# Three product kinds in three passes: the order of the matmuls in a split-precision weight unit

## The chip, the core and the metric

The kernel runs on one core of a Trainium2 chip. Its engines are TensorE (PE, matrix products, with its weight loads listed as PEld), VectorE (DVE), ScalarE (ACT), GpSimd (POOL) and SyncE (SP, which issues the DMAs). The metric is the device time of one execution in microseconds. Matrix products read their operands from SBUF, the on-chip memory, and write to PSUM banks.

## The reference

Two transformer-like blocks, one after the other, on 256 tokens of width 2048, all in float32. Cut to its matrix products:

```python
def first_block(x, ...):
    h = rms_norm(x, mix_norm)
    parts = split(h @ w_in)                    # inputs of three mixers, and gates
    y_a, y_b, y_c = s5_mixer(...), hgrn2_mixer(...), mlstm_mixer(...)
    merged = sum(sigmoid(g_i) * (y_i @ w_branch_i))
    x = x + merged @ w_out
    x = x + conv_ffn(rms_norm(x, ffn_norm), ffn_w_up, ffn_conv_w, ffn_conv_b, ffn_w_down)
    return rms_norm(x, final_norm)

def second_block(x, ...):
    proj = rms_norm_2(x, g_mix) @ w_in         # inputs of two attentions, and gates
    x = x + (g[0] * (o_a @ w_o_mla) + g[1] * (o_b @ w_o_dil)) @ w_o
    gt, up = split(rms_norm_2(x, g_ffn) @ w_gate_up)
    return x + (silu(gt) * up) @ w_down
```

The up projections have 88 column tiles of 128 (5632 x 2), the down projections 44 tiles of depth.

## The kernel before

Activations lie transposed in SBUF, 16 tiles (KT) of 128 features by 256 tokens. Weights are streamed through a ring of four slots (RING). One "unit" is the 16 tiles of 128x128 that give one output tile of 128 features; its result is accumulated in one PSUM bank. SP loads a slot when PE has signalled `consumed` for it.

Part of the products are made in a split form. A float32 weight w is rounded to `w_high` (a reduced format, fp32r) by ACT in `round_weights` (line 909, copy at line 913; semaphore `rounded`), and the rest, `w_low` = w - `w_high`, is written over the slot by DVE (`lower_weights`, line 1303) or in a few cases by POOL (semaphore `lowered`). The activations have a high and a low part as well. For each tile PE then adds three products to the bank, in `mm3` (line 486): high weight with high activation, high weight with low activation, low weight with high activation. That is 48 matmuls for one unit, each with a weight load of its own. ACT and DVE prepare weights two units ahead of PE (AHEAD).

Split units come from `unit_split` (line 465), called with a body that `project_split` (line 493) makes. It is used for the first 10 units and 6 rounds of four of the mixers' projection, for w_out (4 rounds), for the up projection (4 units and 21 rounds), for the first 26 units of the second block's input projection (in2), for w_o (4 rounds), and for the second up projection (4 units and 21 rounds): 268 units. The projections that give tokens by features (`tokens`, line 522) and the down projection (`down`, line 586) have loops of their own, with the three products of a tile together.

The unit after a norm is special (`after_norm`, line 504): mix, up, in2 and up again. There the activations are being made while PE could begin. DVE scales 16 tiles (`normalise_split`, line 1319); ACT rounds them in five groups (`round_input`, line 924), whose bounds are `H_GROUPS` (line 61); POOL makes the low parts of the first three groups (`lower_input`, line 1951; H_POOL = 3), DVE those of the other two. Before the first tile of each group PE waits for that group's low part.

In the first block's up projection, DVE also does a short convolution on every result (`conv_pairs`, line 1796), ACT applies Silu, and DVE multiplies the two halves of a pair. In its first 17 rounds of four units ACT also rounds each product to `acts_high` (line 1120) after waiting for it, before it goes on to the next two weight units (`conv_round`, line 1122), and POOL makes `acts_low`. One unit in each such round (POOL_TURN) has its `w_low` made by POOL (`lower_round`, line 1968).

Each engine runs its own program in order; a wait holds up whatever stands behind it on that engine. On SP, DVE, ACT and POOL nothing is changed.

Of the kernel before, what the change touches and what calls it, by code (L numbers as in the profile page):

```python
# [36 lines left out]
P = 128  # L37
# [3 lines left out]
KT = D // P  # L41
# [19 lines left out]
H_GROUPS = [(0, 2), (2, 4), (4, 8), (8, 12), (12, 16)]  # L61
H_POOL = 3
# [119 lines left out]
def build(nc, t, out):  # L182

    with ExitStack() as ctx:
# [36 lines left out]
        w_low = alias("w_low", ring_base, [P, RING, UNIT])  # L221
        w_high = alias("w_high", arena_base, [P, RING, UNIT], 94)
# [54 lines left out]
        bank = [ctx.enter_context(nc.psum_tensor(f"bank{i}", [P, 2, T], F32)) for i in range(8)]  # L277
# [6 lines left out]
        rounded = [sem(f"unit_rounded{s}") for s in range(RING)]  # L284
        lowered = [sem(f"unit_lowered{s}") for s in range(RING)]
# [30 lines left out]
        h_scaled, h_rounded = sem("h_scaled"), sem("h_rounded")  # L316
        h_lowered_pool, h_lowered_vector = sem("h_lowered_by_pool"), sem("h_lowered_by_vector")
# [124 lines left out]
        def _(pe):  # L442
            units = Units(landed, rounded, lowered, consumed, drained)
# [5 lines left out]
            def mm(o, lhsT, rhs, first=True, last=True):  # L449
                return nc.tensor.matmul(o, lhsT, rhs, start=first, stop=last)  # L450
# [13 lines left out]

            def unit_split(body):
                s, _, _, _, free = units.next(split=True)
                pe.wait_ge(lowered[s], units.lowered[s].value())
                if not isinstance(free, int) or free > 0:
                    pe.wait_ge(drained[s], free)
                body(s).then_inc(consumed[s], 1)  # L470
# [15 lines left out]
            def mm3(o, s, c, high, low, first, last):  # L486

                c = slice(c * P, (c + 1) * P)
                mm(o, w_high[:, s, c], high, first, False)
                mm(o, w_high[:, s, c], low, False, False)  # L490
                return mm(o, w_low[:, s, c], high, False, last)

            def project_split(high, low, waits=None):
                def body(s):
                    for k in range(KT):
                        if waits:
                            waits(k)
                        last = mm3(bank[s][:, 0], s, k, high[:, k], low[:, k], k == 0, k == KT - 1)
                    return last
                return body  # L500

# [2 lines left out]
            def after_norm(high, low):  # L504

                n = splits[0]
                splits[0] += 1

                def waits(k):
                    for g, (first, _) in enumerate(H_GROUPS):  # L510
                        if k == first and g < H_POOL:
                            pe.wait_ge(h_lowered_pool, H_POOL * n + g + 1)
                        elif k == first:
                            pe.wait_ge(h_lowered_vector, (len(H_GROUPS) - H_POOL) * n + g - H_POOL + 1)
                unit_split(project_split(high, low, waits))

            def project(s):
                for k in range(KT):
# [102 lines left out]
            for g in range(2):  # L621
                for k in range(KT):
                    last = mm(bank[7][0:ML, g], w_if[:, k, g * ML:(g + 1) * ML], hT[:, k], k == 0, k == KT - 1)
# [4 lines left out]
            for part in range(2):  # L628
                s = take()
                if part:  # L630
                    pe.wait_ge(qk_ready, 1)
                for h in range(ML):
                    for o, q0, q1, e in PIECES[h]:
                        for n, (k, _, _, _) in enumerate(PIECES[h]):
                            c = (2 * h + n) * ML_DH + e
                            last = mm(bank[4 + o // 2][q0:q1, o % 2], ring[:, s, c:c + q1 - q0], CA[:, k],
                                      n == 0, n == 1)
# [8 lines left out]
            for h in range(ML):  # L646
                last = mm(bank[5 + h // 2][:, h % 2], spread(h, ML), rows[:, 3])
# [3 lines left out]
            for h in range(ML):  # L651
                last = mm(bank[5 + h // 2][:, h % 2], spread(h, ML), rows[:, 5])
            last.then_inc(cast_done, 1)
            pe.wait_ge(cast_taken, 2)
            for h in range(ML):
                for b in range(TB):
                    for n, (k, p0, p1, _) in enumerate(PIECES[h]):
                        last = mm(bank[4 + h][:, b, b * P:T], KH[p0:p1, k, b * P:(b + 1) * P],
                                  QH[p0:p1, k, b * P:T], n == 0, n == 1)
# [3 lines left out]
            for h in range(ML):  # L663
                mm(bank[4 + h // 2][:, h % 2], ones[:], PM[:, h, 0:T], True, False)
                last = mm(bank[4 + h // 2][:, h % 2, P:T], ones[:], PM[:, h, T:T + P], False, True)
# [3 lines left out]
            for h in range(ML):  # L669
                for k, p0, p1, e in PIECES[h]:  # L670
                    c = h * ML_DH + e
                    mm(bank[4 + k // 2][p0:p1, k % 2], vals[:, 0, c:c + p1 - p0], PM[:, h, 0:T], True, False)
                    last = mm(bank[4 + k // 2][p0:p1, k % 2, P:T], vals[:, 1, c:c + p1 - p0],
                              PM[:, h, T:T + P], False, True)
# [10 lines left out]
            for lvl in range(9):  # L685
# [4 lines left out]
                for h in range(HG):  # L690
                    if lvl == 8:
                        last = mm(bank_row[4 + h // 4][:, h % 4 * P:(h % 4 + 1) * P], X[:, h, 0:P], X[:, h, P:T])
                    else:
                        for b in range(TB):
                            c = slice(b * P, (b + 1) * P)
                            last = mm(bank[4 + h // 2][:, h % 2, c], (X if lvl else HK)[:, h, c],
                                      (X if lvl else HQ)[:, h, c])
# [4 lines left out]
            for h in range(HG):  # L702
                mm(bank[4 + h // 2][:, h % 2, 0:P], VN[:, 0, h], PD[:, h, 0:P])
                mm(bank[4 + h // 2][:, h % 2, P:T], VN[:, 0, h], PO[:, h], True, False)
                last = mm(bank[4 + h // 2][:, h % 2, P:T], VN[:, 1, h], PD[:, h, P:T], False, True)
# [12 lines left out]
            for n in range(S5_STATES):  # L718
# [3 lines left out]
                last = mm(bank[4 + n % 4][:, 0], ring[:, sre, c], MT[:, U0 + n // 4])  # L722
                if n == S5_STATES - 1:
                    last.then_inc(consumed[sre], 1)
                last = mm(bank[4 + n % 4][:, 1], ring[:, sim_, c], MT[:, U0 + n // 4])
# [5 lines left out]
            for f in range(S5_TILES):  # L731
                pe.wait_ge(s5_states, f + 1)
                for part, (slot, st) in enumerate(((cre, SR), (cim, SI))):
                    for n in range(4):
                        c = (4 * f + n) * P
                        last = mm(bank[4 + f][:, part], ring[:, slot, c:c + P], st[:, 4 * f + n], n == 0, n == 3)
# [3 lines left out]
            s = take()  # L740
            for f in range(S5_TILES):
                for k in range(S5_TILES):
                    c = (f * S5_TILES + k) * P
                    last = mm(bank[4 + f // 2][:, f % 2], ring[:, s, c:c + P], GA[:, k], k == 0, k == 3)
# [1445 lines left out]
```

## Time and profile before

| | us |
|---|---|
| median of 3 runs | 3418.73 |
| lowest, highest | 3416.93, 3419.38 |
| the profiled execution | 3416.97 |
| its span, first to last instruction | 3415.2 |

| engine | busy us | share of the span |
|---|---|---|
| PE | 3251.1 | 95% |
| DVE | 1558.3 | 46% |
| ACT | 1158.9 | 34% |
| POOL | 244.7 | 7% |

The profile's page gives totals; the trace behind it gives each instruction's start and duration, and behind each idle time of an engine the instruction that ended it, in square brackets with the microseconds of idle time. In a timeline, matmuls of one kind in a row are one line, so split units, in which three kinds alternate, have a line for each matmul. A matmul's duration overlaps that of the next; the time it costs is the distance between starts. TensorE's clock is granted at full or half rate (2.4 or 1.2 GHz); PEclk is its mean over a stretch.

### The profile page before, as it was taken

What the parts mean: (1) busy time and instruction counts of PE and PEld (TensorE: products, weight loads), DVE (VectorE), ACT (ScalarE), POOL (GpSimd) and SP (SyncE); (2) the same over time, 40 slices, a digit from 0 to 9 for tenths busy, and PEclk for the clock granted to TensorE, in tenths of its full rate; (3) what the DMA queues carried; (4) which work ended last, traced back from release to release, by engine and by line L of the source; (5) the groups of instructions that cost most, each with busy time, mean ns of one, the idle gap of its engine ahead of it and who ended that gap; (6) DMA issues with size and microseconds to landing.
All of it is one profiled execution on the core that took longest, in us unless ns stands there. A gap on an engine that the chain in (4) does not pass through costs nothing. (4 is left out here: it accounts for less than half of the span.)

```text
span 3415.2 us, 53946 instructions
## 1 busy us (share of the span) xinstructions
PE 3251.1 (95%) x22512; PEld 3035.8 (89%) x22512; DVE 1558.3 (46%) x1764; ACT 1158.9 (34%) x1127; POOL 244.7 (7%) x148
## 2 busy tenths in 40 slices
PE   7999989999998999999997999999999999999999
PEld 7897777887898999999996987778889999999999
DVE  5651242942347666675446422312124544444443
ACT  4452101100134444433333332234113445543332
POOL 0000000000002222221000040000000100000000
PEclk8999899999999999999998999999999999999999
DMA  5554222443454555554553553223445455555554
GB/s 186 186 186 139 93 81 89 158 147 133 139 183 146 174 172 174 176 188 158 185 186 113 184 183 134 99 87 108 138 148 172 148 184 184 185 185 176 181 186 168
DMA packets 79704, 533.01 MB, mean 156 GB/s; under 512 B 8976, under 2 KB 9232, under 8 KB 26768
## 3 DMA queue, kind: packets, MB, share of 16 engines
q1 hardware_dynamic: 79632, 531.99, 45.8%
q8 instruction: 53, 0.87, 0.1%
q14 instruction: 19, 0.16, 0.0%
HBM read 529.85 MB, written 2.10 MB: 156 GB/s over the span
## 5 line engine op out<-in xcount | busy, mean ns | idle before, releaser
L1299 DVE TENSOR_TENSOR w_low<-ring,w_high 128x2048 fp32r<-128x2048 f32 (+1 forms) x386 | 853.2, 2211 | 794.9 <-ACT w_high L913 794.6
L450 PE MATMUL bank<-h_low,w_high 128*128 128x256 f32 x3328 | 937.5, 282 | 0.0
L913 ACT ACTIVATE w_high<-ring 128x2048 fp32r<-128x2048 f32 (+1 forms) x416 | 723.0, 1746 | 550.2 <-DMA ring<-in_w_down 316.4
L450 PE MATMUL bank<-up_high,w_high 128*128 128x256 f32 x2816 | 796.7, 283 | 37.4 <-POOL h_low L1949 21.2
L450 PE MATMUL bank<-up_high,w_low 128*128 128x256 f32 x2816 | 791.3, 281 | 0.0
L450 PEld LDWEIGHTS bank<-h_low,w_high 128*128 128x128 f32 x3328 | 632.9, 190 | 0.0
L450 PEld LDWEIGHTS bank<-up_high,w_high 128*128 128x128 f32 x2816 | 533.8, 190 | 42.0 <-issue 35.7
L450 PE MATMUL bank<-hT,ring 128*128 128x256 f32 x2560 | 569.8, 384 | 0.0
L450 PEld LDWEIGHTS bank<-hT,ring 128*128 128x128 f32 x2560 | 491.1, 193 | 74.9 <-issue 7.2
L450 PEld LDWEIGHTS bank<-up_high,w_low 128*128 128x128 f32 x2816 | 533.2, 189 | 0.0
L450 PE MATMUL bank<-acts_high,w_high 128*128 128x256 f32 x1408 | 396.7, 282 | 6.2 <-DVE w_low L1299 5.3
L450 PE MATMUL bank<-acts_high,w_low 128*128 128x256 f32 x1408 | 397.7, 282 | 0.0
L450 PE MATMUL bank<-acts_low,w_high 128*128 128x256 f32 x1408 | 396.3, 281 | 0.0
L450 PE MATMUL bank<-arena,ring 128*128 128x256 f32 (+1 forms) x1408 | 308.1, 384 | 10.9 <-ACT arena L1103 4.7
L450 PEld LDWEIGHTS bank<-arena,ring 128*128 128x128 f32 (+1 forms) x1408 | 265.8, 191 | 52.9 <-issue 10.2
L450 PEld LDWEIGHTS bank<-acts_high,w_high 128*128 128x128 f32 x1408 | 265.1, 188 | 6.8 <-DVE w_low L1299 5.7
L450 PEld LDWEIGHTS bank<-acts_high,w_low 128*128 128x128 f32 x1408 | 271.0, 192 | 0.0
L450 PEld LDWEIGHTS bank<-acts_low,w_high 128*128 128x128 f32 x1408 | 265.5, 189 | 0.0
L1299 DVE TENSOR_TENSOR arena<-arena 128x1024 f32 (+7 forms) x176 | 171.6, 983 | 34.6 <-ACT arena L1107 12.9
L450 PE MATMUL bank<-mix_high,w_high 128*128 128x256 f32 x544 | 155.3, 285 | 15.9 <-POOL mix_low L1949 14.0
L450 PE MATMUL bank<-mix_high,w_low 128*128 128x256 f32 x544 | 155.2, 285 | 0.0
L450 PE MATMUL bank<-mix_low,w_high 128*128 128x256 f32 x544 | 154.7, 284 | 0.0
(219 smaller groups left out, 3314.4 us busy)
## 6 DMA issues: line engine op xcount, KB each, us to landing
ring<-in_w_up SPq DMA_DIRECT2D x176, 1024.0 KB, 4.8
ring<-in_w_down SPq DMA_DIRECT2D x128, 704.0 KB, 4.0
ring<-in_w_in SPq DMA_DIRECT2D x66, 1024.0 KB, 4.8
ring<-in_w_mix SPq DMA_DIRECT2D x62, 1024.0 KB, 4.9
ring<-in_w_gates SPq DMA_DIRECT2D x48, 1024.0 KB, 4.9
ring<-in_w_branch SPq DMA_DIRECT2D x16, 1024.0 KB, 4.8
ring<-in_w_out SPq DMA_DIRECT2D x16, 1024.0 KB, 4.8
ring<-in_w_o SPq DMA_DIRECT2D x16, 1024.0 KB, 4.8
```

The source lines that it names most:

```text
L450: return nc.tensor.matmul(o, lhsT, rhs, start=first, stop=last)
L913: A(w_high[:, s, 0:cols], ring[:, s, 0:cols], ACT.Copy).then_inc(rounded[s], 1)
L1299: return V.tensor_tensor(o, a, b, op)
```

## The change

A unit's 16 tiles are passed through three times, one product kind in each pass. In ordinary units: high weights with high activations, high weights with low activations, then a wait for the unit's low weights, then low weights with high activations. The wait at the unit's start is for `rounded` instead of `lowered`. In the unit after a norm the first pass waits for each group's rounding instead of its low part, the second pass uses the low weights, and the third waits for each group's low part. The order of the sum in the bank changes, its terms don't. `tokens` and `down` keep `mm3`.

```diff
@@ unit_split
-                pe.wait_ge(lowered[s], units.lowered[s].value())
+                pe.wait_ge(rounded[s], units.rounded[s].value())
@@ project_split
-            def project_split(high, low, waits=None):
+            def tile(k):
+                return slice(k * P, (k + 1) * P)
+
+            def project_split(high, low):
+
                 def body(s):
+                    o = bank[s][:, 0]
                     for k in range(KT):
-                        if waits:
-                            waits(k)
-                        last = mm3(bank[s][:, 0], s, k, high[:, k], low[:, k], k == 0, k == KT - 1)
+                        mm(o, w_high[:, s, tile(k)], high[:, k], k == 0, False)
+                    for k in range(KT):
+                        mm(o, w_high[:, s, tile(k)], low[:, k], False, False)
+                    pe.wait_ge(lowered[s], units.lowered[s].value())
+                    for k in range(KT):
+                        last = mm(o, w_low[:, s, tile(k)], high[:, k], False, k == KT - 1)
                     return last
                 return body
@@ after_norm
-                def waits(k):
-                    for g, (first, _) in enumerate(H_GROUPS):
-                        if k == first and g < H_POOL:
-                            pe.wait_ge(h_lowered_pool, H_POOL * n + g + 1)
-                        elif k == first:
-                            pe.wait_ge(h_lowered_vector, (len(H_GROUPS) - H_POOL) * n + g - H_POOL + 1)
-                unit_split(project_split(high, low, waits))
+                starts = [a for a, _ in H_GROUPS]
+
+                def body(s):
+                    o = bank[s][:, 0]
+                    for k in range(KT):
+                        if k in starts:
+                            pe.wait_ge(h_rounded, len(H_GROUPS) * n + starts.index(k) + 1)
+                        mm(o, w_high[:, s, tile(k)], high[:, k], k == 0, False)
+                    pe.wait_ge(lowered[s], units.lowered[s].value())
+                    for k in range(KT):
+                        mm(o, w_low[:, s, tile(k)], high[:, k], False, False)
+                    for k in range(KT):
+                        if k in starts:
+                            g = starts.index(k)
+                            if g < H_POOL:
+                                pe.wait_ge(h_lowered_pool, H_POOL * n + g + 1)
+                            else:
+                                pe.wait_ge(h_lowered_vector, (len(H_GROUPS) - H_POOL) * n + g - H_POOL + 1)
+                        last = mm(o, w_high[:, s, tile(k)], low[:, k], False, k == KT - 1)
+                    return last
+                unit_split(body)
```

## Rows read from the trace of the kernel before

**Rows 1.** The page, part 1: busy time, share and instructions by engine.
```profile
PE 3251.1 (95%) x22512; PEld 3035.8 (89%) x22512; DVE 1558.3 (46%) x1764; ACT 1158.9 (34%) x1127; POOL 244.7 (7%) x148
```

**Rows 2.** Page groups (idle before, releaser), then PE's waits: total us, times, longest.
```profile
L450 PE MATMUL bank<-up_high,w_high 128*128 128x256 f32 x2816 | 796.7, 283 | 37.4 <-POOL h_low L1949 21.2
...
PE bank L450 <- POOL h_low L1949: 28.4, 6, 7.8
...
PE bank L450 <- POOL w_low L1949: 16.2, 15, 1.1
PE bank L450 <- POOL mix_low L1949: 14.0, 2, 11.2
...
PE bank L450 <- POOL in_low L1949: 10.7, 2, 7.9
```

**Rows 3.** One stretch of the second up projection: us, busy and instructions by engine.
```profile
2664.50:3150.50 486.00, 486.00 (x4129) 486.00 (x4128) 215.54 (x130) 230.51 (x196) 25.12 (x34) 1.00 0.54 184
```

**Rows 4.** Timeline of PE in the second down projection: start us, us, instruction.
```profile
3186.50 0.28 PE L450 MATMUL bank<-acts_high,w_low 128*128 128x256 f32 x1
3186.62 0.28 PE L450 MATMUL bank<-acts_high,w_high 128*128 128x256 f32 x1
```

**Rows 5.** Timeline, ACT's fifth rounding in mix, up, in2, up2; DVE's low groups (up).
```profile
31.04 1.06 ACT L928 ACTIVATE mix_high<-hT 128x1024 fp32r<-128x1024 f32 x1 [2.67 <-DVE hT L1296]
...
1038.05 1.06 ACT L928 ACTIVATE up_high<-hT 128x1024 fp32r<-128x1024 f32 x1 [2.62 <-DVE hT L1296]
...
1852.49 1.06 ACT L928 ACTIVATE in_high<-hT 128x1024 fp32r<-128x1024 f32 x1 [2.67 <-DVE hT L1296]
...
2659.04 1.06 ACT L928 ACTIVATE up_high<-hT 128x1024 fp32r<-128x1024 f32 x1 [2.62 <-DVE hT L1296]
...
1037.94 2.43 DVE L1299 TENSOR_TENSOR h_low<-hT,up_high 128x1024 fp32r<-128x1024 f32 x2
```

**Rows 6.** Timeline of PE: last restart after each norm, and the next unit's first matmul.
```profile
34.39 0.58 PE L450 MATMUL bank<-mix_high,w_high 128*128 128x256 f32 x1 [1.88 <-DVE mix_low L1299]
...
39.11 0.28 PE L450 MATMUL bank<-mix_high,w_high 128*128 128x256 f32 x1
...
1036.60 0.58 PE L450 MATMUL bank<-up_high,w_high 128*128 128x256 f32 x1 [2.81 <-POOL h_low L1949]
...
1043.36 0.28 PE L450 MATMUL bank<-up_high,w_high 128*128 128x256 f32 x1
...
1851.04 0.58 PE L450 MATMUL bank<-in_high,w_high 128*128 128x256 f32 x1 [2.87 <-POOL in_low L1949]
...
1856.87 0.28 PE L450 MATMUL bank<-in_high,w_high 128*128 128x256 f32 x1
...
2657.59 0.58 PE L450 MATMUL bank<-up_high,w_high 128*128 128x256 f32 x1 [2.81 <-POOL h_low L1949]
...
2664.49 0.27 PE L450 MATMUL bank<-up_high,w_high 128*128 128x256 f32 x1
```

**Rows 7.** Timeline of ACT in one round of the first up projection.
```profile
1159.53 0.42 ACT L1120 ACTIVATE acts_high<-arena  x1 [7.20 <-DVE arena L1299]
...
1161.26 3.72 ACT L913 ACTIVATE w_high<-ring 128x2048 fp32r<-128x2048 f32 x2
...
1172.26 3.70 ACT L913 ACTIVATE w_high<-ring 128x2048 fp32r<-128x2048 f32 x2
...
1183.48 0.42 ACT L1120 ACTIVATE acts_high<-arena  x1 [7.21 <-DVE arena L1299]
```

**Rows 8.** Timeline of DVE in the same round.
```profile
1172.51 0.54 DVE L1811 TENSOR_SCALAR arena<-bank,vec 128x256 f32<-128x256 f32 x1 [0.71 <-PE bank L450]
...
1175.99 4.98 DVE L1299 TENSOR_TENSOR w_low<-ring,w_high 128x2048 fp32r<-128x2048 f32 x1 [1.68 <-ACT w_high L913]
```

**Rows 9.** Timelines of POOL and of PE in the same round.
```profile
1174.24 4.59 POOL L1949 TENSOR_TENSOR w_low<-ring,w_high 128x2048 fp32r<-128x2048 f32 x1 [0.95 <-ACT w_high L913]
...
1178.96 0.38 PE L450 MATMUL bank<-up_high,w_high 128*128 128x256 f32 x1 [1.08 <-POOL w_low L1949]
```

## What was predicted

> **What bounds the kernel now.** I read the page's head first: TensorE (PE) is busy 95% of the span and the next engine, VectorE (DVE), 46% [rows 1]. A PE-bound kernel can be shortened in two ways only, by less PE work or by less PE idle time. The change keeps every matmul and every weight load, so only idle time is in play. Next I read what PE waited for [rows 2], keeping only the waits on low parts that this change touches: POOL's low part of the normalised input (21.2 us of the 28.4 under h_low, in the two up projections; the other 7.2 are the merges before w_out, whose wait stays where it was), 14.0 for the first norm, 1.9 behind DVE there [rows 6], 10.7 for in2, and 16.2 us in 15 waits for a weight unit whose low part POOL makes. Those 64.0 us (1.9%) are the most that the edit can be aimed at. The question is how much of it comes back later.
>
> The rate in the steady stretches is in [rows 3]: 486 us hold 4129 matmuls with no idle time, 0.1177 us each, so a unit of 48 takes 5.65 us and one pass of 16 takes 1.88 us.
>
> **The reordering itself.** In 268 units (34 mix, 16 w_out, 88 up, 26 in2, 16 w_o2, 88 up2) the same 48 products run in another order. Each matmul has its own weight load before and after, and in the even stretch of [rows 3] all three kinds alternate without a gap. So I cost the order at 0. Bound from both sides: a timeline's start is given to 0.01 us [rows 4]; if the neighbour mattered by a tenth of that, 1 ns for each of 12,864 matmuls, it would be 13 us either way, and I give that little weight.
>
> **The added wait in the middle of the unit.** A unit now has three waits (rounded, bank drained, lowered) instead of two. The nearest row is in the down stage, which already waits in the middle of a unit (for acts_lowered, three matmuls into every fourth unit): the matmuls on its two sides start 0.12 us apart, as everywhere [rows 4]. A wait that is already satisfied therefore costs 0 on that row; the upper bound is the restart of a wait that is not satisfied, whose first matmul holds 0.38 instead of 0.28 us [rows 9], 0.1 x 268 = 27 us. I take 0. Queued behind the new wait are PE's own matmuls only; ScalarE (ACT), DVE and SP wait for PE's unit end, as before.
>
> **The four first units after a norm.** Here is the step that I think is counter-intuitive. The old order runs 12 matmuls for each group of four tiles as soon as that group's low part is there. The new order runs 4, then must wait for the last group to be rounded, and only then has work for good: 4 matmuls of the last group, 16 of w_low, 16 of the low parts, 36 in all. Before, PE's last restart in the two up norms and in in2 also had exactly 36 matmuls left: it came when POOL's third group landed (1036.60, 1851.04, 2657.59) [rows 6]. Now it comes when ACT has rounded the fifth group, which ends at 1038.05 + 1.06 = 1039.11, 1853.55 and 2660.10 [rows 5]; with 0.15 us from a release to the matmul (the first restart of [rows 9] follows POOL's end, 1174.24 + 4.59 = 1178.83, by 0.13) that is 1039.26, 1853.70 and 2660.25. So the last 36 matmuls start **2.66 us later** than before, in each of the three, though PE starts its first matmul about 1.6 us earlier. DVE's two low groups of the up norm end at 1037.94 + 2.43 = 1040.37 [rows 5], before the low pass begins (20 matmuls after 1039.26, at 1041.6 at the earliest), so nothing else is late.
>
> How long do the 36 take? From the last restart to the next unit's first matmul, before: 1043.36 - 1036.60 = 6.76, 1856.87 - 1851.04 = 5.83, 2664.49 - 2657.59 = 6.90 us [rows 6]; the spread is how soon after the restart PE's clock rises from 1.2 to 2.4 GHz. I take their mean, 6.5. Then the next unit starts at 1045.8 instead of 1043.36 (+2.4), at 1860.2 instead of 1856.87 (+3.3), at 2666.75 instead of 2664.49 (+2.3). Bounds: 36 x 0.1177 = 4.2 us at full clock throughout and 8.5 at half of it throughout; the three rows span 5.8 to 6.9.
>
> The first norm differs: DVE puts a weight unit ahead of its two low groups, so the old order restarted last at 34.39 with 24 matmuls left and the next unit began at 39.11. The new one restarts when ACT's fifth rounding ends, 31.04 + 1.06 = 32.10, at 32.25 with 36 left, and ends at 38.75: **-0.4** (bounds -1.0 to 0.0 from the same spread).
>
> The Trainium skill ("TensorE: Matmul & The Clock Gate", "What's actually happening") says that the half-rate clock is the default and that activity releases it; by it, the thinner first pass of the new order can only keep the clock low longer. If the 36 ran wholly at half rate, the sum would be about 1 to 2 us worse for each norm.
>
> **The first up projection (conv FFN, split activations).** The largest single target is here: 15 gaps of 1.25 us beyond the normal spacing, 18.7 us by start times (16.2 by the page's count), one per round of four units. A round lasts 23.95 us, and 4 x 5.65 = 22.6 would be PE's own. But who sets 23.95? I followed ACT and DVE through one round [rows 7, 8]. ACT rounds an activation tile at 1159.53 (released by DVE), loads a table, rounds two weight units from 1161.26; DVE lowers them and does the convolution of the round's first two units back to back, its product releases ACT's next rounding of activations, and ACT rounds the next two weight units from 1172.26 to 1175.96; DVE lowers the second of these from 1175.99 (4.98 us, beside POOL's 4.59) and its product releases ACT at 1183.48, where the round closes: 1183.48 - 1159.53 = 23.95. PE appears once in it: DVE waits 0.71 us for a bank at 1172.51, but then waits 1.68 us for ACT before 1175.99, so that wait is not on the loop. The loop of ACT and DVE runs at 23.95 us without PE, and PE is carried along. Speeding PE up does not shorten a round; it only lets PE run nearer to its inputs, once.
>
> How near: the unit that POOL lowers (ready at 1178.83) may start up to two passes, 3.76 us, before it; it started at 1178.96, so it can start at 1175.2 (its high part is rounded at about 1174.1). PE gains 1.35 us a round until there, about three rounds, then waits as much as before, split between ACT's high part of the pair's first unit (rounded at 1161.26 + 1.86 = 1163.1; that unit starts 2 x 5.65 + 1.25 = 12.55 us before 1178.96, at 1166.4, a lead of 3.2) and POOL's low part in mid-unit. So the stage gives **-3.75 us**, not -18.7. After the last such round PE waits for nothing until the down projection, so the lead is kept; and the round's first DVE work after the norm waits for PE's second unit, so the +2.4 of the norm moves the whole loop: +2.4 - 3.75 = **-1.35** for norm and stage.
>
> The other stages (mix, w_out, in2, w_o2, up2) show no wait on a weight's low part in [rows 2], so the later wait gives 0 there.
>
> **Sum.** -0.4 (mix norm) - 1.35 (first up) + 3.3 (in2) + 2.3 (up2) = **+3.9 us**. The last two pass through in full, because PE waits for no weights from there on to the end of their projections. On the profiled execution (3416.97 us for a span of 3415.2) it is 3420.9; the median of the runs is 1.8 us above that execution, so the forecast is 3418.73 + 3.9 = 3422.6, rounded to 3422.5.
>
> **Rivals.**
> (a) The loop of ACT and DVE does feel PE. Then all 15 gaps vanish: -18.7 in place of -3.75, 15 us below my forecast, **3407.5**. For it: the waits name POOL's w_low as the releaser, and the new order gives 3.76 us of cover for a 1.25 us wait. Against: the slack of 1.68 us behind DVE's only wait for PE, and DMA loads that are landed before ACT asks. 13%.
> (b) The mid-unit wait is not free. Where PE's weight load behind the wait is not started ahead, each of the 268 units shows a hole of 0.1 us (the restart's extra in [rows 9]): +27 us, **3449**. It decides from 0.03 us per unit on. Against: [rows 4], and the normal spacing at unit starts, which carry waits. The Trainium skill (the same page, "Step-by-step: what each phase is for") says that the queue pulls a weight load ahead of matmuls in flight; a wait on that load would forbid it, and by that rule a hole is expected. The trace does not agree at the waits that exist. 6%.
> (c) PE can't keep its lead in the first up projection (the lead is used up by another wait, such as the rounding of the activations' last part before the down projection): the norms' delays remain alone, 3.9 + 3.75 = +7.6, **3426.5**, slower by 0.22%. 11%.
> (d) The change doesn't do what it says, because the wait on the high part is met no earlier than that on the low part: everything stays, **3419**. The first norm's rows speak against it. 5%.
> My forecast: 65%. Own range, with each 36-matmul stretch at 5.8 to 7.7 us and the lead at 3.2 to 3.9: 3419 to 3426.
>
> **Chances and range.** A measurement of this kernel can tell about 0.2%, 6.8 us, from no change. Faster: (a) alone, 0.13. Slower: (b), most of (c), and the upper tail of my case when the clock rises late in all norms, 0.17. Within 0.2%: 0.70. For 8 in 10, the range takes in (c) and reaches up to (a): 3407 to 3430.
>
> **What would show it.** After the change: (1) the waits of PE on h_low, mix_low and in_low are gone in the four norm units and waits on ACT's high parts stand there, with a last restart at ACT's fifth rounding; (2) the unit after the norm starts 2 to 3.5 us later in in2 and up2, counted from ACT's fifth rounding; (3) in the first up projection rounds still last 23.95 us, and PE's idle time there is 10 to 15 us, now in two waits a round, on ACT's w_high and POOL's w_low; rounds of 22.6 us would prove (a); (4) matmuls on both sides of the mid-unit wait start 0.12 us apart in up2; 0.2 or more would prove (b). The forecast fails most simply if (3) is wrong, since that term is the largest.

## The result: 0.42% slower, and the profile after

The changed kernel takes 3432.25 us (median of 5 runs, 3431.11 to 3433.91) against 3418.73 (5 runs, 3414.76 to 3421.47): ratio 1.0042, 95% interval 1.0027 to 1.0056, that is +13.5 us. Forecast was 3422.5 (+3.9), so the time lies outside the range of 3407 to 3430, by 2.25 us.

The page of the changed kernel: its span, then busy time by engine, then PE's costliest group.

```profile
span 3429.3 us, 53946 instructions
...
PE 3268.3 (95%) x22512; PEld 3047.5 (89%) x22512; DVE 1557.1 (45%) x1764; ACT 1158.2 (34%) x1127; POOL 245.3 (7%) x148
...
L450 PE MATMUL bank<-up_high,w_high 128*128 128x256 f32 x2816 | 373.6, 285 | 30.3 <-ACT up_high L949 24.4
```

The number of matmuls is the same as in [rows 1], but PE is busy 17.2 us longer. The span grew by 14.1 us, so the time outside PE's busy time even fell by 3.1 us. So the loss is not idle time, which was all that the forecast reckoned with. (The busy times of single kinds can't be compared with those of before, since overlapping matmuls of one kind in a row are counted once.)

PE's waits in the changed kernel: total us, times, longest.

```profile
PE bank L450 <- ACT up_high L949: 24.4, 8, 6.1
...
PE bank L450 <- ACT mix_high L949: 15.2, 4, 9.0
PE bank L450 <- ACT in_high L949: 12.4, 4, 6.2
...
PE bank L450 <- ACT w_high L934: 5.9, 12, 0.5
...
PE bank L450 <- POOL w_low L1970: 3.0, 12, 0.3
```

Against [rows 2], the waits for low parts became waits for rounding by ACT: 21.2, 14.0 + 1.9 and 10.7 us turned into 24.4, 15.2 and 12.4. The 16.2 us behind POOL's low weights are 8.9 us now, in two kinds.

The first unit after the norm before up, PE's timeline in the changed kernel (passes of one kind are one line):

```profile
1040.78 1.22 PE L450 MATMUL bank<-up_high,w_high 128*128 128x256 f32 x4 [2.47 <-ACT up_high L949]
1041.80 3.62 PE L450 MATMUL bank<-up_high,w_low 128*128 128x256 f32 x16
1045.21 2.60 PE L450 MATMUL bank<-h_low,w_high 128*128 128x256 f32 x16
1047.65 1.60 PE L450 MATMUL bank<-up_high,w_high 128*128 128x256 f32 x12
```

The last restart is ACT's fifth rounding, with 36 matmuls left, and the next unit starts 6.87 us later; in the kernel before it was 6.76 us after a restart that came earlier [rows 6].

Late in the first up projection, the same view:

```profile
1423.09 2.10 PE L450 MATMUL bank<-up_high,w_low 128*128 128x256 f32 x16 [0.25 <-POOL w_low L1970]
...
1431.38 2.18 PE L450 MATMUL bank<-up_high,w_high 128*128 128x256 f32 x16 [0.50 <-ACT w_high L934]
```

Two waits a round, one at the start of a unit for ACT and one in mid-unit for POOL. ACT's loop in the changed kernel, for one round as in [rows 7]:

```profile
1187.88 0.42 ACT L1141 ACTIVATE acts_high<-arena  x1 [7.24 <-DVE arena L1320]
...
1211.86 0.42 ACT L1141 ACTIVATE acts_high<-arena  x1 [7.24 <-DVE arena L1320]
```

A round lasts 23.98 us (1211.86 less 1187.88), against 23.95 before. The loop kept its pace.

The surprise is in stretches without any wait. One unit in up2, and one in in2:

```profile
2681.42 2.08 PE L450 MATMUL bank<-up_high,w_high 128*128 128x256 f32 x16
2683.34 2.05 PE L450 MATMUL bank<-h_low,w_high 128*128 128x256 f32 x16
2685.22 2.05 PE L450 MATMUL bank<-up_high,w_low 128*128 128x256 f32 x16
2687.10 2.08 PE L450 MATMUL bank<-up_high,w_high 128*128 128x256 f32 x16
```

```profile
1860.18 2.08 PE L450 MATMUL bank<-in_high,w_high 128*128 128x256 f32 x16
1862.10 2.08 PE L450 MATMUL bank<-in_low,w_high 128*128 128x256 f32 x16
1864.02 2.05 PE L450 MATMUL bank<-in_high,w_low 128*128 128x256 f32 x16
1865.90 2.08 PE L450 MATMUL bank<-in_high,w_high 128*128 128x256 f32 x16
```

The distance between starts is 1.92 us for some passes (0.120 us a matmul) and 1.88 for others (0.1177, the rate of [rows 3]). A unit takes 5.687 us in up2 and 5.720 in in2, instead of 5.653. In up2 the pass of high weights with high activations is slow; in in2 also that with low activations. What the slow ones share is that both operands lie in the large tensor called the arena; h_low lies in the tensor hT and w_low in the weight ring.

By starts of the same unit in the two profiled executions, the 14.1 us between the spans divide as follows ("again" is a second profile of the same changed kernel, below):

| term | forecast | changed | again |
|---|---|---|---|
| unit after the norm: mix | -0.4 | -0.8 | -0.1 |
| the same, up | +2.4 | +2.7 | +3.2 |
| first up projection (lead) | -3.75 | -2.9 | -2.8 |
| unit after the norm: in2 | +3.3 | +1.9 | +0.4 |
| the same, up2 | +2.3 | +2.6 | +1.4 |
| other ordinary units (spacing) | 0 | +7.6 | +6.5 |
| stretches that no edit touches | 0 | +3.0 | +5.4 |

The spacing of the ordinary units is the same in both profiles. The column "again" has less in that row because the first unit of w_out, which starts behind a wait, took 7.29 us there instead of 8.47 (8.48 in the kernel before).

### The profile page after: what moved, and what is told of

The parts are those of the page before. It is cut to its first block and busy times, and to the rows that moved or that the text cites. A ratio compares the mean times of both kernels' runs of the same rounds, so it can differ in the third digit from the quotient of the medians.

```text
span 3429.3 us, 53946 instructions
## 1 busy us (share of the span) xinstructions
PE 3268.3 (95%) x22512; PEld 3047.5 (89%) x22512; DVE 1557.1 (45%) x1764; ACT 1158.2 (34%) x1127; POOL 245.3 (7%) x148
## 5 line engine op out<-in xcount | busy, mean ns | idle before, releaser
L450 PE MATMUL bank<-h_low,w_high 128*128 128x256 f32 x3328 | 428.2, 280 | 0.0
L450 PEld LDWEIGHTS bank<-h_low,w_high 128*128 128x128 f32 x3328 | 410.3, 189 | 0.0
L450 PE MATMUL bank<-up_high,w_high 128*128 128x256 f32 x2816 | 373.6, 285 | 30.3 <-ACT up_high L949 24.4
L450 PEld LDWEIGHTS bank<-up_high,w_high 128*128 128x128 f32 x2816 | 353.0, 193 | 35.7 <-ACT up_high L949 14.4
L450 PE MATMUL bank<-up_high,w_low 128*128 128x256 f32 x2816 | 364.1, 283 | 3.0 <-POOL w_low L1970 3.0
L450 PEld LDWEIGHTS bank<-up_high,w_low 128*128 128x128 f32 x2816 | 346.5, 191 | 5.4 <-POOL w_low L1970 5.4
L1970 POOL TENSOR_TENSOR w_low<-ring,w_high 128x2048 fp32r<-128x2048 f32 (+1 forms) x30 | 137.4, 4584 | 243.2 <-ACT w_high L934 243.2
L450 PE MATMUL bank<-arena 128*128 128x128 f32 (+4 forms) x496 | 106.0, 372 | 38.2 <-DVE arena L1664 19.6
L1141 ACT ACTIVATE acts_high<-arena x68 | 28.4, 418 | 317.3 <-DVE arena L1320 317.3
```

What stands on the lines that cost most here:

```text
L1141: A(acts_high[:, bass.ds(n, 1)], ACTS[:, bass.ds(n, 1)], ACT.Copy).then_inc(acts_rounded, 1)
L1970: return nc.gpsimd.tensor_tensor(low, whole, high.bitcast(F32), ALU.subtract)
```

## The experiments

Times are medians; each comparison is with the kernel before on the same chip (3416.26, 3416.73, 3416.25 and 3416.34 us in the four sets).

**The ordinary units alone.**

```diff
             def after_norm(high, low):
...
-                            pe.wait_ge(h_rounded, len(H_GROUPS) * n + starts.index(k) + 1)
-                        mm(o, w_high[:, s, tile(k)], high[:, k], k == 0, False)
...
+                                pe.wait_ge(h_lowered_pool, H_POOL * n + g + 1)
...
+                        last = mm3(bank[s][:, 0], s, k, high[:, k], low[:, k], k == 0, k == KT - 1)
```

> The ordinary units in three passes with the late wait, the four units after a norm as in the kernel before. My theory after reading the changed kernel's trace: each pass in which both operands lie in the arena costs 2.2 ns more for each matmul, so units in mix and in2 take 5.720 us, in w_out, up, w_o2 and up2 5.687 us, against 5.653 before, in all +7.6 us outside the first up projection; there PE still gains a one-time lead of 3.75 us less 0.7 us of slower matmuls. Sum +4.6 us (+0.13%), apart from up to 3 us by which the clock differs between executions in stages that no edit touches. A rival, that the slower matmuls come from the new units after the norms (the clock), expects units of 5.653 us here and a kernel 3 us faster than before.

Measured: 3425.22, ratio 1.0023 (1.0014 to 1.0033), +9.0 us where +4.6 was expected. The stretch from the second in2 unit to the end of the in2 units, and that from the second up2 unit to the end (stretch, us, busy and matmuls, granted clock, DMA share, GB/s), first here, then in the kernel before:

```profile
1859.50:2003.10 143.60, 143.15 (x1202) 1.00 0.54 183
2670.80:3166.40 495.60, 494.85 (x4178) 1.00 0.53 182
```

```profile
1857.00:1998.80 141.80, 141.37 (x1201) 1.00 0.54 185
2664.50:3157.30 492.80, 491.99 (x4178) 1.00 0.54 183
```

At full clock and without waits the same work takes 1.8 and 2.8 us longer, with the old units after the norms. The spacing comes from the order in the ordinary units; the rival (clock after the norms) falls. By unit starts, 4 us of the profiled execution's +9.1 are in stretches that no edit touches, which is about the excess over the expectation.

**The units after a norm alone.**

```diff
             def project_split(high, low):
...
-                        mm(o, w_high[:, s, tile(k)], high[:, k], k == 0, False)
...
+                        last = mm3(bank[s][:, 0], s, k, high[:, k], low[:, k], k == 0, k == KT - 1)
```

> Only the four units after a norm are changed (first pass on rounded groups, then low weights, then low parts); the ordinary units keep three products for each tile and wait for the low weights at their start. My theory: the last restart of each of these units comes with ACT's fifth rounding, 2.66 us later than before in up, in2 and up2, so the unit after it begins 2 to 2.7 us later there and 0.8 us earlier in mix, in all +6.4 us (+0.19%); spacing 0.1177 us as before; the first up projection keeps its 15 gaps of 1.25 us, since PE has no lead to take. Rival: earlier first matmuls pay, so the kernel is faster by 1 to 4 us.

Measured: 3424.32, ratio 1.0022 (1.0012 to 1.0031), +8.1 us, whose interval (+4 to +11) holds the +6.4. The rival, which expected a gain, falls. The same two stretches, then PE's wait in the first up projection:

```profile
1860.80:2002.70 141.90, 141.42 (x1201) 1.00 0.55 185
2669.70:3162.50 492.80, 491.98 (x4178) 1.00 0.54 183
```

```profile
PE bank L450 <- POOL w_low L1966: 16.1, 15, 1.1
```

The spacing is that of before, and the 15 waits are back. The two halves add to 17.1 us where the whole is 13.5, within the uncertainty of the three.

**Pairs.**

```diff
+                    for k in range(KT):
+                        mm(o, w_high[:, s, tile(k)], high[:, k], k == 0, False)
+                        mm(o, w_high[:, s, tile(k)], low[:, k], False, False)
+                    pe.wait_ge(lowered[s], units.lowered[s].value())
+                    for k in range(KT):
+                        last = mm(o, w_low[:, s, tile(k)], high[:, k], False, k == KT - 1)
```

> The ordinary units in two passes: for each tile high x high and high x low one after the other, then, behind the wait for the low weights, the 16 low weights. Units after a norm as before. This tells what makes matmuls slower. Theory S (both operands move on by a tile at each matmul while both lie in the arena): here each high weight is loaded twice in a row, so the spacing is 0.1177 us everywhere, and the kernel is faster than before by the lead alone, -3.75 us. Theory R (it is enough that both operands lie in the arena for many matmuls in a row): the pairs of mix and in2 run at 0.120 us (unit 5.72 us, +4 us in all), those of up2 at 0.1177 because h_low lies outside the arena; the kernel is equal to before. In both, rounds of the first up projection keep 23.95 us until the unsplit rounds.

Measured: 3409.74, ratio 0.9981 (0.9972 to 0.9991), 6.5 us faster than before, where theory S expected 3.75 us and theory R none.

```profile
1851.10:1994.70 143.60, 143.11 (x1201) 1.00 0.53 183
2659.30:3148.10 488.80, 487.95 (x4178) 1.00 0.54 185
```

In in2 it is as slow as three passes (143.6), as theory R said: high weights twice in a row don't help while everything lies in the arena. But up2 became faster than the kernel before (488.8 against 492.8), which neither theory had. So the place of the operands matters, and by more than "arena or not". PE's waits in the first up projection were 7.4 us for ACT's w_high and 5.2 for POOL's w_low, 13 each, so the lead is taken and then held, as with three passes.

**The weights moved by 832 bytes**, the three-pass kernel otherwise as it is.

```diff
-        w_high = alias("w_high", arena_base, [P, RING, UNIT], 94)
+        w_high = nc.alloc_sbuf_tensor_at("w_high", [P, RING, UNIT], R32, offset=arena_base + 94 * T * 4 + SHIFT * 4)
```

> The changed kernel with w_high moved by 832 bytes in each partition, so that its offset within 1024 bytes is that of the ring and of h_low instead of that of the other arena tensors; the scratch tiles behind it move along. Theory A (alignment of the two operands decides): in mix and in2 both passes on w_high go back to 0.1177 us (unit 5.653), while in up2, w_out and w_o2 the high pass becomes 0.1177 and the pass with h_low becomes 0.120 (unit stays 5.687); the kernel is 4 us faster than the changed one. Theory R' (the region of the memory decides, not the alignment): nothing changes, units 5.720 and 5.687 us, the time of the changed kernel.

Measured: 3390.53, ratio 0.9914 (0.9897 to 0.9931): 25.7 us faster than before and 42 faster than the changed kernel (of another set), where 4 were expected. One unit of up2, then of in2:

```profile
2700.25 1.98 PE L452 MATMUL bank<-up_high,w_high 128*128 128x256 f32 x16
2702.06 2.06 PE L452 MATMUL bank<-h_low,w_high 128*128 128x256 f32 x16
2703.96 2.00 PE L452 MATMUL bank<-up_high,w_low 128*128 128x256 f32 x16
```

```profile
1859.87 1.98 PE L452 MATMUL bank<-in_high,w_high 128*128 128x256 f32 x16
1861.68 1.98 PE L452 MATMUL bank<-in_low,w_high 128*128 128x256 f32 x16
1863.49 1.98 PE L452 MATMUL bank<-in_high,w_low 128*128 128x256 f32 x16
```

1.81 us a pass is 0.1133 us a matmul, which no 48 matmuls in a row of the kernel before reached (at least 0.1175 us each). Theory A (the operands' addresses decide) has the right kind of cause and far too small a size; that the region decides is refuted, since the region is the same.

**The distance measured.** A distance is the activations' address less the weights', in bytes within one partition.

```diff
-            rounds_split(21, project_split(up_high, h_low))
+            rounds_split(21, probe(up_high, [0, 64, 128, 192]))
...
+                    for n in range(3 * KT):
...
+                        k = n % KT
+                        m = (k % (KT - 1)) * T + d
+                        last = mm(o, (w_low if whole else w_high)[:, s, tile(k)], flat[:, m:m + T],
+                                  n == 0, n == 3 * KT - 1)
```

> A measuring kernel, whose output isn't the reference's: in the rounds of six stages every unit runs 48 matmuls of one kind, and the activations are read from an address moved by a fixed number of bytes, another one for each of the four units of a round (up2: 0, 64, 128, 192; up: 256 to 448; w_out: 512 to 704; w_o2: 768 to 960; mix: 16, 32, 48, 96, all with w_high; in2 with w_low, whose own distance is 192 bytes: 0, 320, 640, 832 added). The distance is the activations' offset less the weights', within 1024 bytes. Theory D, that the distance between the two operands' offsets alone sets the spacing: 0 gives 0.1199 us, 192 gives 0.1133, 832 gives 0.1179, and in2 with nothing added (distance 192) gives the value of up2 with 192 added, in2 with 832 added (distance 0) that of up2 with 0. Rival: the order of kinds and the regions matter more; then the units with w_low differ from those with w_high at equal distance by 2 ns or more, and the 16 distances show no pattern.

The four units of one round in up2 (w_high, 0, 64, 128, 192 added), and of one in in2 (w_low, 0, 320, 640, 832 added, that is distances 192, 512, 832, 1024):

```profile
2905.41:2911.16 5.75, 5.75 (x51) 1.00 0.54 182
2911.16:2916.81 5.65, 5.65 (x50) 1.00 0.54 186
2916.81:2922.51 5.70, 5.70 (x51) 1.00 0.54 184
2922.51:2927.98 5.47, 5.47 (x50) 1.00 0.58 192
...
1904.89:1910.35 5.46, 5.46 (x50) 1.00 0.57 192
1910.35:1916.09 5.74, 5.74 (x50) 1.00 0.52 183
1916.09:1921.75 5.66, 5.66 (x51) 1.00 0.53 185
1921.75:1927.51 5.76, 5.76 (x50) 1.00 0.56 182
```

Each unit needs some matmuls to settle, so the spacings are taken from the starts in its second and third pass. They are 120.0, 117.8, 118.7 and 113.3 ns for 0, 64, 128 and 192, and w_out with 512 to 704 and w_o2 with 768 to 960 repeat them (120.0, 117.8, 118.7, 113.3). So the pattern of these four repeats every 256 bytes, and in2 gives the same values with other weights in another tensor: 113.3 at 192, 120.0 at 512, 117.8 at 832, 120.0 at 1024. There the fast unit has nothing added to the activations' address, while in up2 the unit with nothing added is the slow one, so it is the distance and not that address. Theory D holds in these 16 units, with one exception: in the first of in2's six rounds the unit at distance 192 took 5.65 us (117.8 ns a matmul), in the other five 5.46. The instructions and the addresses were the same.

**The kernel before with w_high moved, and pairs with w_high moved** (the edits above, combined).

> The kernel before, with nothing changed but the place of w_high (832 bytes further). If the offsets alone sped up the shifted three-pass kernel, this one gains as well: units of 5.44 us in mix and in2 (distance 192 for all three kinds) and about 5.55 us in w_out, w_o2 and up2 (two kinds at 192, one at 0), the first up projection at its 23.95 us a round; -25 us against the kernel before. If passes are needed for it, units stay at 5.65 us and the time stays within 4 us of before.

Measured: 3402.5, ratio 0.9963 (0.9948 to 0.9977), 14 us faster, where 25 were expected. In2 gained (136.6 us for the stretch of 141.8), up2 not at all:

```profile
1846.90:1983.50 136.60, 136.16 (x1201) 1.00 0.57 192
2650.30:3143.00 492.70, 491.95 (x4177) 1.00 0.54 183
```

In up2, products at distances 192, 0 and 192 alternate, and the sequence runs at 117.8 ns, not at the mean of what the parts run at alone (115.5); in w_out the same sequence ran at 119.2 (units of 5.72 us).

> Ordinary units in two passes (pairs of high x high and high x low, then the low weights behind their wait), units after a norm as before, w_high moved by 832 bytes. If both effects add: the gain of the kernel before with the moved w_high, and PE's one-time lead of 3.2 to 3.75 us in the first up projection: -28 us against before. If the lead is eaten by another wait: no faster than the kernel before with the moved w_high.

Measured: 3378.99, ratio 0.9888 (0.9872 to 0.9905), 37.7 us faster, where 28 were expected. Units of up2 take 5.560 us: the stretch is 8 us shorter than in the kernel before with w_high moved, which the expectation didn't have. The lead of the first up projection is kept as well, so both effects are there.

**All distances 192.** w_high moved by 832 bytes and hT, with h_low, by 192.

```diff
+        sb("pad_before", [P, 48])
         hT = sb("hT", [P, KT, T])
         hT_base = nc.sbuf_base - KT * T * 4
+        sb("pad_behind", [P, 16])
```

> The kernel before, with w_high moved by 832 bytes and the normalised input (hT and its low part) by 192, so that the activations of every product kind stand 192 bytes from its weights within 256. Theory D (the distance decides, period 256 bytes): all split units take 5.44 us in the loops, -15 us against the kernel before with w_high moved alone. Rival (three kinds in turn hold the spacing at 117.8 ns by themselves): units of w_out, w_o2 and up2 stay at 5.65 us.

> The changed kernel with the same two shifts. If the order of the matmuls cost something only through the distance of their operands, the units take 5.44 us here too, and against the kernel before with the same shifts there remain the two other terms: +6.4 us from the units after the norms and about -3 us from the lead in the first up projection, so +3.4 us. Rival (the order costs by itself): the passes run slower than the kernel before does, by the 7.6 us of the unshifted pair, in all +11 us.

> The same two shifts, ordinary units in two passes (pairs, then the low weights), units after a norm as before: the lead of 3.2 to 3.75 us without the cost of the norms. It should be 3 us faster than the kernel before with the same shifts, and 10 to 14 us faster than the two-pass kernel with w_high moved alone.

| kernel | us | ratio to before (95%) |
|---|---|---|
| order of before | 3378.49 | 0.9892 (0.9875 to 0.9908) |
| three passes | 3368.15 | 0.9869 (0.9845 to 0.9893) |
| pairs | 3372.63 | 0.9877 (0.9856 to 0.9899) |

The up2 stretch of the three, in this order, for the second one with its in2 stretch ahead (columns as above):

```profile
2639.60:3113.80 474.20, 473.43 (x4178) 1.00 0.55 190
```

```profile
1835.20:1977.10 141.90, 141.48 (x1202) 1.00 0.53 185
2641.90:3116.10 474.20, 473.41 (x4178) 1.00 0.55 190
```

```profile
2636.00:3110.20 474.20, 473.38 (x4177) 1.00 0.55 190
```

In up2 all three orders take 474.2 us, 18.6 less than before. So in that stretch the order by itself costs nothing; in the changed kernel it cost 2.2 ns for each matmul at distance 0 because of where the tensors happened to lie. The second kernel's in2 stretch shows something else: all distances are 192 there as well, and yet it ran at 117.8 ns. The order isn't the reason: the three-pass kernel with w_high moved has the same order and the same distances in in2 and took 136.6 us for the stretch.

The expected differences between the three did not come out. The second was to be 3.4 us slower than the first and is 10 us faster by the medians; the third was to be 3 us faster than the first and is 6; the intervals overlap. Single executions of these three spread over 3360.8 to 3384.5 us, where the kernel before spreads over 3414.7 to 3421.4 in the same set. The two profiles show where the first and the second part. These are the last 19 units of the first up projection, where PE waits for nothing, and the second down projection, whose code and operand addresses are the same in both; first the order of before, then three passes:

```profile
1442.05:1549.46 107.41, 107.41 (x914) 1.00 0.50 176
3113.90:3364.20 250.30, 248.66 (x2111) 1.00 0.52 176
```

```profile
1437.35:1540.71 103.36, 103.36 (x915) 1.00 0.53 183
3116.20:3357.40 241.20, 239.84 (x2111) 1.00 0.54 183
```

That is 4.0 and 9.1 us in favour of the three passes, against 5.4 in in2 the other way (141.9 against 136.5), at full clock and at distance 192 on both sides. In the first up projection the kernel with the order of before had begun at 5.44 us a unit; in the fourth of the 21 rounds of this loop it went over to 5.65 and stayed there.

**Finer distances, and passes in a row.**

> A measuring kernel, whose output isn't the reference's: units of 48 products of one kind with the activations read at a chosen distance from the weights, as in the first of its kind, now in finer steps (up: 208, 224, 240, 248; w_out: 160, 176, 80, 16; w_o2: 0, 16, 32, 48; in2: 4, 8, 12, 24; mix: 144, 40, 96, 112), and in up2 with the distance changed from pass to pass: 64-192-192, 0-192-192, 128-192-192, 192-64-192. In the changed kernel the pass at distance 192 that follows one at 64 ran at 117.7 ns, where 113.1 was measured alone. Theory L (the state of the pass before carries over): 192 after 64 stays at 117.7, 192 after 0 or 128 falls to 113. Theory D alone: every pass at 192 runs at 113.

By spacing inside the passes, both measuring kernels taken together: 112 bytes was fast in the one stage where it was tried (113.3 ns, mix). 16 bytes was fast in mix (113.3, but 116.5 in the first round), 116.8 in w_out (but 113.3 in the first round) and 118.7 in w_o2. 32 gives 116.4 to 116.6; 48, 160, 208 and 224 give 118 to 119.5 in nearly all rounds; 24, 40, 80 and 96 give about 120; and 4 gives 123.2. Of the distances tried in more than one stage, only 192 was fast in each, apart from the first round of in2. In up2, the pass at 192 right behind one at 64, 0 or 128 took 113.8 to 114.6 ns and the next one 113.3, so theory L as I put it falls; but in the unit 192-64-192 the first pass took 113.3 and the last 117.5, so theory D alone falls too. The same distance has two rates, then, and which one it takes depends on more than the distance of the pass just before.

**The changed kernel again.**

> The changed kernel once more, to part what the change does from what differs between executions. In its first profile the stretch of norms and gates behind in2, which no edit touches, took 3.3 us longer than in the kernel before (87.4 against 84.1 us), with more half-rate clock in it. If that is chance, it is between 84.0 and 87.4 us here and the spacings are exactly as before (units of 5.720 and 5.687 us). If it belongs to the change, it is 87.4 us again. The whole: +7.6 (spacing) + 6.4 (units after norms) - 2.9 (lead) = +11 us against before, and up to 3 more from the clock.

Measured: 3430.93, ratio 1.0042 (1.0028 to 1.0056), +14.6 us, where 11 to 14 were expected. Units take 5.720 and 5.687 us again. The untouched stretch behind in2, in the kernel before, in the changed one and in the changed one again:

```profile
2098.14:2182.20 84.06, 84.06 (x364) 0.96 0.29 100
```

```profile
2103.12:2190.47 87.35, 87.35 (x364) 0.92 0.28 96
```

```profile
2105.56:2191.31 85.75, 85.75 (x365) 0.94 0.29 98
```

It changes with the clock granted (0.96, 0.92, 0.94), between profiles of one and the same kernel. Over all fourteen profiles, in which no edit touches this stretch, it took about 84.1 us six times, 85.8 six times and 87.4 twice. The two of 87.4 (the changed kernel and the second measuring kernel) have the new units after the norms, but so do three of those of 84.1.

## Why the prediction was wrong, point by point

**Bounds of the kernel.** Right as far as it went: PE-bound, same matmuls. The conclusion "only idle time is in play" was the error. The rate of PE is a second quantity, and an edit that keeps all matmuls can move it.

**The reordering itself, costed at 0: the step that failed.** It measured +7.6 us in the profiled pair, the largest term of all. The prediction had bounded it ("1 ns for each of 12,864 matmuls ... 13 us either way") and then gave the bound little weight, and left it out of the forecast's own range. The reason given was that "all three kinds alternate without a gap". The even spacing in [rows 3] was read as a property of a matmul; it is a property of the sequence. The trace lists the next matmul's weight load beside the running matmul, and the rate goes with the distance between the addresses of activations and weights, within 256 bytes: 120.0 ns at 0, 113.3 at 192. By what path inside the chip the two meet, the runs don't show. In the kernel before, kinds at distances 0, 64 and 192 took turns (0, 0 and 192 in mix and in2), and the sequence ran at 117.8. Taken apart into passes, the kinds at distance 0 ran at their own 120, while the low weights at 192 did not reach 113.3: they ran at 117.7, the slower of the two rates that this distance has. So the order lost on the one side and gained nothing on the other. The Trainium skill says of weight loads ("TensorE: Matmul & The Clock Gate", "Step-by-step: what each phase is for"): "Loading the next tile's weights doesn't steal SBUF read bandwidth from the running matmul." If that were all, the place of the operands would not matter. The runs here do not agree: with the same products and loads, 192 bytes of distance change the spacing by 6%.

**The mid-unit wait, costed at 0.** Right. In up2 the pass before it lasts 1.88 us from start to start, as [rows 3] give it, and so does the pass behind it; and the aligned three-pass kernel needs the same 474.2 us as the aligned kernel without the wait. Rival (b) had the right sign for a wrong reason; the loss per unit was 0.03 to 0.07 us where it said 0.1, and the hole that it asked for is not there.

**Units after a norm.** The mechanism held in all four: the last restart moved to ACT's fifth rounding with 36 matmuls left, which took 6.87 us in up. The terms +2.4, +3.3, +2.3 and -0.4 measured +2.7, +1.9, +2.6 and -0.8, then +3.2, +0.4, +1.4 and -0.1 in the second profile. The sum is +6.4 and +4.8, forecast +7.6. The last 36 matmuls took 6.1 to 7.0 us in one profile and 5.7 to 6.9 in the other, against 6.5 in the forecast, at a granted clock of 0.58 to 0.60 in the three later norms of the first profile (0.59 to 0.72 before); none ran at half rate throughout. So the sizes of single norms were partly luck. The second sign, units 2 to 3.5 us late in in2 and up2, held in one of the four cases, up2 of the first profile; in2 came close to it there, and both fell short in the second. Alone, the edit cost +8.1 us (+4 to +11). The forecast's own range has a slip that decided nothing: by its own bounds its upper end is about 3427, not 3426.

**First up projection.** Right in kind, against rival (a): 15 waits of POOL shrank, but the loop of ACT and DVE kept its pace and PE took its lead once. Forecast -3.75, measured -2.9 and -2.8 (by unit starts); about 0.7 us of the difference is the slower spacing of the 20 units behind the last held round. I had said 10 to 15 us of waits would remain; it was 8.9 by the page's count, which sees less of two short waits than of a long one. Rival (c), in which the lead is lost, did not occur.

**What is not explained.** Three of the 14 us (five in the second profile) lie in stretches that no edit touches and go with the granted clock there. Single executions of one kernel differ by as much, and the edit of units alone had 4 us of it, the edit after the norms hardly any in its profile. Whether the change makes those stretches slower on average, by moving them against the clock's changes, or whether these profiles happened to fall so, was not settled. Without them, by an estimate from the two medians and this row, the kernel would have taken about 3429 us: outside the forecast's own range (to 3426) because of the order's 7.6 us, but inside the wide one of 3407 to 3430.

## What to carry to other kernels

When an edit reorders matmuls without changing them, put a price on the rate and not only on the waits: a rate measured in an interleaved sequence is no property of its members. Where PE is the bound, look at the addresses of the two operands; moving one tensor by some hundred bytes was worth 14 us in the order of before and 42 in three passes, where covering 18.7 us of visible waits gave back 2.9. And ask of a wait, before removing it, whether the releaser's own loop contains the waiting engine; if not, removing it bought one lead and no more here.

## What the runs showed of the hardware that was not expected

- With 128x256 matmuls of this kind, each with its weight load, PE's spacing depends on the distance between activations and weights with a period of 256 bytes: 0: 120.0, 64: 117.8, 128: 118.7, 192: 113.3 ns, at full clock and with no wait. The values at 0, 64 and 192 were the same for two weight tensors, and all four for three activation tensors.
- Sequences of several distances don't run at the mean of their members: 0, 64 and 192 in turn ran at 117.8 (mean 117.0), 192, 0 and 192 in turn at 117.8 in up2 and 119.2 in w_out (mean 115.5).
- At distance 192 there are two rates, 113.3 and 117.8 ns, for the same instructions at the same addresses: first and later rounds of in2 in the first measuring kernel (5.65 and 5.46 us a unit), and one loop of the aligned kernel of before (5.44 and then 5.65 us). The second down projection took 241.2 or 250.3 us in kernels in which all its distances are 192 and its code is the same, and the aligned kernels' executions spread over some 20 us. What picks the rate stays open, and so does the fastest arrangement; the fastest single execution was 3360.8 us, with pairs and all distances 192.
